# Grouped attention: which engine copies the transposed probabilities out of PSUM for units with two key tiles

## The chip, the cores and the metric

The kernel runs as one program on one core of a Trainium2 chip. The metric is the device time of that core in microseconds (us), lower is better. The core has five engines that matter here, each with its own in-order instruction queue: TensorE (PE, with its weight loads shown apart as PEld), VectorE (DVE), ScalarE (ACT), GpSimd (POOL) and SyncE (SP, which only issues transfers). They hand work to one another through semaphores: an instruction waits until a counter has reached a value, and adds to another counter when it is done.

## The reference, cut to what matters

The reference chains two small transformers of two layers each over 256 tokens of width 1024. The second one begins with a grouped-query attention layer (`gqa_axial_mixer`): 16 query heads share 4 key and value heads of width 64. The 256 tokens attend to 512 keys (256 of a context and their own 256); the 256 context tokens attend to the 256 context keys alone.

```
s = jnp.einsum('bqkgd,bskd->bkgqs', qi, k_all).astype(jnp.float32) * ATTN_SCALE
p = jax.nn.softmax(s, axis=-1).astype(v_all.dtype)
return jnp.einsum('bkgqs,bskd->bqkgd', p, v_all)
...
sc = jnp.einsum('bqkgd,bskd->bkgqs', qc, kc).astype(jnp.float32) * ATTN_SCALE
pc = jax.nn.softmax(sc, axis=-1).astype(vc.dtype)
oc = jnp.einsum('bkgqs,bskd->bqkgd', pc, vc).reshape(b, lc, A_WIDTH)
yc = (oc * jax.nn.silu(zc)) @ w_out
```

## The kernel before, in words

The whole kernel is one list of instructions for each engine, written out in order by hand; the layers follow each other, and nothing is scheduled at run time but by the semaphores. Four attention layers run through the same functions, named `attention` once in each engine's list, with a stage name: "l0", "l1", "a" (the grouped one, the only one that the change touches) and "b".

`attn_units(s)` cuts a stage into units. In stage "a" a unit is one pair of heads (t, from 0 to 7), one block of 128 queries (qt, 0 or 1) and one region: region 0 is the tokens, with 512 keys, four key tiles of 128; region 1 is the context, with 256 keys, two key tiles. The order is: for each t, for each qt, region 0 and then region 1. So there are 32 units; the even ones have four key tiles and the odd ones two. A job is the two units (qt 0 and 1) of one t and one region: units 12 and 14 are one job, units 13 and 15 the next. `AU0` and `AJ0` are the numbers of a stage's first unit and job among all stages.

A unit passes through these steps, each one or more rounds n after the other:

- PE, round n: two score products of unit n into PSUM tile A (`scores_a`, line 984).
- DVE, round n: the negated row maximum of unit n (line 1197), counted by `at_mx`.
- ACT, round n: two exponentials of unit n from PSUM into one of three SBUF buffers (tiles ATP, RSQ and HSQ, by unit modulo 3; line 1874), with row sums, counted by `at_ex`.
- DVE, round n + 1: `scaled`: a reciprocal of the sums (line 1172) and two multiplications of the probabilities (line 1182), counted by `at_p`.
- PE, round n + 2: `turn`: the transposes of the probabilities, 128 by 128 each, four or eight in all, into the PSUM tensor `RO` (tile R; line 636), counted by `at_t`. Before it PE waits that the unit's `at_p` is there and that the unit before has been copied out of `RO` (`at_tc`), for there is one `RO` for all units.
- ACT, round n + 2, ahead of the exponentials of unit n + 2: the copy of `RO` to SBUF (line 1863), to tile ATT for region 0 and to a part of tile B for region 1, counted by `at_tc`.
- PE, round n + 3, for the second unit of a job: the products with the values into PSUM tile G (`value_a`, line 993); in stage "a" they stand after that round's `turn`.
- DVE, round n + 4, for the second unit of a job: `out_a`, the product with the gate (line 1721); POOL then splits it into two parts for the next product.

Within a round PE's order is scores, `turn`, values; DVE's is maximum, `scaled`, `out_a`; ACT's is copy, exponentials.

Of the kernel before, what the change touches and what calls it, by code (L numbers as in the profile page):

```python
# [19 lines left out]
ACT = mybir.ActivationFunctionType  # L20
# [3 lines left out]
P = 128  # L24
# [87 lines left out]
AU0, AJ0 = {}, {}  # L112
# [7 lines left out]
def attn_units(s):  # L120

    out = []
    if s in ("l0", "l1"):
        for p in range(8):
            for qt in range(2):
                out.append((p, qt, qt + 1, p, qt == 1))
    else:
        regions = 2 if s == "a" else 1
        for t in range(8):
            for qt in range(2):  # L130
                for r in range(regions):
                    out.append((t, 2 * r + qt, 4 if r == 0 else 2, t * regions + r, qt == 1))
    return out


def program(nc, x_tok, wst, wmod, vec, cst, x_t, ctx_t, p_t, pos, pos4, tab, rpb, lam4, grow, y_t):
    with ExitStack() as ctx:
# [3 lines left out]
        def sem(name):  # L141
            return ctx.enter_context(nc.semaphore(name))
# [106 lines left out]
        def att(s, j):  # L249

            if s == "l0":
                return ATT[:, j % 2, 0:2, :].unsqueeze(1)
            if s == "l1":
                return ATT[:, j % 2, :, :].rearrange("p (l k) q -> p l k q", l=2)
            if j % 2 == 0:
                return ATT[:, :, :, :]
            spare = B[:, 4096:6144] if s == "a" else mv[:, 12288:14336]
            return spare.rearrange("p (l k q) -> p l k q", l=2, k=4)

        def lanes(a, nk):  # L260

            return AA[:, 1024 * (a % 2):1024 * (a % 2) + 1024].rearrange("p (l k) -> p l k", l=2)[:, :, 0:nk * P]
# [8 lines left out]
        def small(at, a, n):  # L271

            return SM[:, at + 2 * (a % 3):at + 2 * (a % 3) + n]
# [13 lines left out]
        def bc(ap, n):  # L287
# [4 lines left out]
        RO = ctx.enter_context(nc.psum_tensor("R", [P, 1024], F32))  # L292
# [21 lines left out]
        at_s, at_b, at_mx, at_ex, at_rc, at_lm, at_pa, at_p, at_t, at_tc, at_pv, at_g, at_oh, at_o = (  # L314
            sem("at_s"), sem("at_b"), sem("at_mx"), sem("at_ex"), sem("at_rc"), sem("at_lm"), sem("at_pa"), sem("at_p"),
            sem("at_t"), sem("at_tc"), sem("at_pv"), sem("at_g"), sem("at_oh"), sem("at_o"))
# [26 lines left out]
        n = 0  # L343
# [6 lines left out]
        n = 0  # L350
# [17 lines left out]
        def evacuated(eng, u):  # L368

            eng.wait_ge(bank_free[u % 2], u // 2 + 1)  # L370
# [732 lines left out]
        def _(dv):  # L1103
            v = nc.vector
# [60 lines left out]
            def scaled(s, n):  # L1165

                units = attn_units(s)
                nk = units[n - 1][2]
                a = AU0[s] + n - 1
                sm, rc = small(92, a, 2), small(98, a, 2)  # L1170
                dv.wait_ge(at_ex, 2 * (a + 1))
                v.reciprocal(rc, sm).then_inc(at_rc, 1)
                dv.wait_ge(at_rc, a + 1)
                if s == "l0":
                    p0, p1 = PRB[a % 3][:, 0, 0:nk * P], PRB[a % 3][:, 1, 0:nk * P]
                    v.tensor_scalar(p1, p1, rc[:, 1:2], LAM, ALU.mult, ALU.mult).then_inc(at_lm, 1)
                    dv.wait_ge(at_lm, a + 1)
                    v.scalar_tensor_tensor(p0, p0, rc[:, 0:1], p1, ALU.mult, ALU.add).then_inc(at_p, 1)
                else:
                    for c in range(2):  # L1180
                        pr = PRB[a % 3][:, c, 0:nk * P]
                        i = v.tensor_scalar(pr, pr, rc[:, c:c + 1], None, ALU.mult)
                        i.then_inc(at_p if c else at_pa, 1)

            def attention(s, bias, take_out=None, first=0, last=None, done=0):
                units = attn_units(s)
                for n in range(first, len(units) + 4 if last is None else last):
                    if n < len(units):
                        a = AU0[s] + n
                        sc = lanes(a, units[n][2])  # L1190
                        dv.wait_ge(at_s, a + 1)
                        b = bias(sc, units[n])
                        if b is not None:
                            biased[0] += 1
                            b.then_inc(at_b, 1)
                            dv.wait_ge(at_b, biased[0])
                        v.tensor_reduce(small(80, a, 2), sc, AX, ALU.max, negate=True).then_inc(at_mx, 1)  # L1197
                    if max(1, done + 1) <= n <= len(units):
                        scaled(s, n)
                    if take_out is not None and n >= 4 and units[n - 4][4]:  # L1200
                        un = units[n - 4]
                        j = AJ0[s] + un[3]
                        dv.wait_ge(at_pv, j + 1)
                        take_out(un, G[j % 2], j)
# [158 lines left out]
            def heads_rest(g):  # L1363

                for tt in range(2):
# [5 lines left out]
                                           ALU.subtract).then_inc(x_lo, 2)  # L1371

            attention("l0", bias_l0, None, 0, 16)
            heads_summed(0)
            attention("l0", bias_l0, None, 16)
            heads_applied(0)
            heads_summed(1)
# [203 lines left out]
            for u, (name, g, kt, panels) in enumerate(TOKEN):  # L1581
# [11 lines left out]
                if u == len(TOKEN) - 1:  # L1593
                    attention("l1", no_bias, None, 0, 2)
                    scaled("l1", 2)
# [71 lines left out]
            for u, (name, g, end) in enumerate(WIDE):  # L1667
# [3 lines left out]
                heads, width = (4, 256) if name == "kv" else (8, 512)  # L1671
# [144 lines left out]
        def _(ac):  # L1816
            act = nc.scalar.activation
# [28 lines left out]
            def load_table(function):  # L1846

                act(SM[:, warmed[0]:warmed[0] + 1], EPSC, function)
                warmed[0] += 1

            def attention(s, out=None, first=0, last=None):
                units = attn_units(s)
                width = 1 if s == "l0" else 2
                for n in range(first, len(units) + 4 if last is None else last):
                    if 2 <= n <= len(units) + 1:
                        p, qt, nk, job, last = units[n - 2]
                        a = AU0[s] + n - 2
                        j = AJ0[s] + job
                        ac.wait_ge(at_t, a + 1)
                        if j >= 2:  # L1860
                            ac.wait_ge(at_pv, j - 1)
                        q = qt % 2
                        act(att(s, j)[:, 0:width, 0:nk, q * P:(q + 1) * P],  # L1863
                            RO[:, :].rearrange("p (l k q) -> p l k q", l=2, k=4)[:, 0:width, 0:nk, :],
                            ACT.Copy).then_inc(at_tc, 1)
                    if n < len(units):
                        nk = units[n][2]
                        a = AU0[s] + n
                        sc = lanes(a, nk)
                        ac.wait_ge(at_mx, a + 1)  # L1870
                        if a >= 3:
                            ac.wait_ge(at_t, a - 2)
                        for c in range(2):
                            act(PRB[a % 3][:, c, 0:nk * P], sc[:, c, :], ACT.Exp, bias=small(80 + c, a, 1),
                                accum_out=small(92 + c, a, 1)).then_inc(at_ex, 1)
                    if n == len(units) and s == "a":
                        evacuated(ac, U0["a_z"] + 7)
                        act(Z2[:, 7, :], Z2[:, 7, :], ACT.Silu).then_inc(z_ok, 1)
                    if n == len(units) + (2 if s == "a" else 0):
                        load_table(ACT.Sqrt)  # L1880
                    if out is not None and n >= 4 and units[n - 4][4]:
                        j = AJ0[s] + units[n - 4][3]
                        ac.wait_ge(at_pv, j + 1)
                        out(units[n - 4], G[j % 2])
# [100 lines left out]
            def heads_out(g):  # L1985

                for tt in range(2):
                    ac.wait_ge(hn_tr, 2 * g + tt + 1)
                    act(XH[:, 8 + 4 * g:12 + 4 * g, tt * P:(tt + 1) * P], A[2 * g + tt].rearrange("p (k t) -> p k t", k=4),
                        ACT.Copy, scale=SUBG).then_inc(x_hi, 2)  # L1990

            attention("l0", out_l0, 0, 18)
            heads_root(0)
            attention("l0", out_l0, 18)
            heads_out(0)
            heads_root(1)
# [178 lines left out]
            for u, (name, g, kt, panels) in enumerate(TOKEN):  # L2175
# [9 lines left out]
                if u == len(TOKEN) - 1:  # L2185
                    attention("l1", None, 0, 2)
# [62 lines left out]
            for u, (name, g, end) in enumerate(WIDE):  # L2249
# [4 lines left out]
                heads, width = (4, 256) if name == "kv" else (8, 512)  # L2254
# [456 lines left out]
```

## Time and profile before

| what | value |
|---|---|
| time, median of 3 runs | 1334.96 us (1333.37 to 1335.37) |
| time of the profiled execution | 1335.48 us |
| its span in the trace | 1333.8 us |
| mean granted TensorE clock | 0.993 of full speed |
| PE, DVE, ACT, POOL busy, share of the span | 96%, 72%, 54%, 31% |
| stage "a", first scores to last transposes | about 963.7 to 1052.8 us of the span |

The span is what the trace covers; the time of the same execution is 1.68 us more. Engine busy times count instructions at work, not their waits. The rows that matter are shown in a section of their own below.

### The profile page before, as it was taken

The page shows a single profiled execution, that of the slowest core. Times are in us where ns is not written, and L with a number is a line of the kernel's source. Part 1 is how long each engine was busy: PE and PEld are TensorE (multiplying, and loading weights), DVE is VectorE, ACT ScalarE, POOL GpSimd, SP SyncE. Part 2 cuts the span into 40 slices and gives each one's busy share as a digit, 9 for nine tenths or more (in the row PEclk, how much of TensorE's full clock was granted, in tenths as well). Part 3 has the DMA queues.
Part 4 walks back from the last instruction along what each step waited for, and adds up shares of the span by engine and source line. Part 5 has one row for each costly group of instructions (what it writes and reads, how often), then busy time and mean ns, then how long its engine had stood idle before and what let it go on. Part 6 is the DMA issues. An engine that isn't in the chain of part 4 may idle for free.

```text
span 1333.8 us, 24373 instructions
## 1 busy us (share of the span) xinstructions
PE 1274.6 (96%) x8896; PEld 1104.8 (83%) x8896; DVE 954.7 (72%) x1426; ACT 720.5 (54%) x1249; POOL 411.8 (31%) x388
## 2 busy tenths in 40 slices
PE   6999999999999999999999999899989999999996
PEld 4887899999988877898999998788855599987656
DVE  6868688888878895558988887854277548453674
ACT  5555455555566777545565557444367515323562
POOL 4942234544433140143455443211012320000022
PEclk9999999999999999999999999899999999999999
DMA  8565246666744443155576664232200274522100
GB/s 308 188 215 179 80 155 224 216 226 209 232 143 143 159 141 95 61 191 174 193 236 212 228 207 146 95 108 85 90 17 1 49 179 137 174 96 79 48 1 32
DMA packets 52665, 191.72 MB, mean 144 GB/s; under 512 B 6048, under 2 KB 6304, under 8 KB 52320
## 3 DMA queue, kind: packets, MB, share of 16 engines
q1 hardware_dynamic: 43488, 158.59, 36.2%
q0 software_dynamic: 8368, 31.33, 7.5%
q8 instruction: 62, 1.02, 0.3%
q10 hardware_dynamic: 720, 0.57, 0.1%
q14 instruction: 27, 0.22, 0.1%
HBM read 189.41 MB, written 1.05 MB: 143 GB/s over the span
## 4 chain that ended last, share of the span: by engine, by line
PE 75%; DVE 11%; ACT 7%; issue 3%; POOL 2%; DMA 1%; SPq 0%; DVEq 0%; ACTq 0%; POOLq 0%
PE G L415 13%; PE G L417 13%; PE G L416 13%; PE A L415 5%; PE A L417 5%; PE A L416 5%; DVE WL L1116 4%; PE R L636 3%; ACT WH L1824 2%; PE R L563 2%; PE R L543 2%; PE R L415 1%; PE R L417 1%; PE R L416 1%; PE A L984 1%
## 5 line engine op out<-in xcount | busy, mean ns | idle before, releaser
L1116 DVE TENSOR_TENSOR WL<-RAW,WH 128x1024 fp32r<-128x1024 f32 x295 | 390.9, 1329 | 251.9 <-ACT WH L1824 251.5
L1824 ACT ACTIVATE WH<-RAW 128x1024 fp32r<-128x1024 f32 x295 | 310.7, 1057 | 394.9 <-PE G L417 282.8
L415 PE MATMUL G<-XH,WH 128*128 128x256 f32 (+1 forms) x1336 | 398.8, 298 | 6.4 <-DVE WL L1116 3.1
L416 PE MATMUL G<-XL,WH 128*128 128x256 f32 (+1 forms) x1336 | 395.5, 296 | 0.0
L417 PE MATMUL G<-XH,WL 128*128 128x256 f32 (+1 forms) x1336 | 395.5, 296 | 0.0
L415 PEld LDWEIGHTS G<-XH,WH 128*128 128x128 f32 x1336 | 256.0, 192 | 19.5 <-issue 8.4
L416 PEld LDWEIGHTS G<-XL,WH 128*128 128x128 f32 x1336 | 256.1, 192 | 7.4
L417 PEld LDWEIGHTS G<-XH,WL 128*128 128x128 f32 x1336 | 256.1, 192 | 6.3
L415 PE MATMUL A<-HH,WH 128*128 128x256 f32 x352 | 99.9, 284 | 1.3 <-POOL HL L2440 1.3
L416 PE MATMUL A<-HL,WH 128*128 128x256 f32 x352 | 99.6, 283 | 0.0
L417 PE MATMUL A<-HH,WL 128*128 128x256 f32 x352 | 99.5, 283 | 0.0
L2416 POOL CAST XH<-HRS 128x256 fp32r<-128x256 f32 x24 | 11.4, 475 | 267.3 <-DVE HRS L1721 267.3
L1197 DVE TENSOR_REDUCE SM<-A 128x2 f32<-128x1024 f32 (+1 forms) x80 | 67.7, 848 | 17.9 <-PE A L984 12.8
L415 PEld LDWEIGHTS A<-HH,WH 128*128 128x128 f32 x352 | 67.5, 192 | 2.9 <-ACT WH L1824 1.9
L415 PE MATMUL G<-WH,XH 128*128 128x512 f32 (+1 forms) x136 | 55.2, 406 | 13.9 <-DVE XL L1142 10.9
L1863 ACT ACTIVATE ATT<-R 128x1024 f32<-128x1024 f32 (+3 forms) x56 | 37.8, 674 | 56.7 <-PE R L636 56.7
L416 PEld LDWEIGHTS A<-HL,WH 128*128 128x128 f32 x352 | 67.5, 192 | 0.1
L417 PEld LDWEIGHTS A<-HH,WL 128*128 128x128 f32 x352 | 67.5, 192 | 0.0
L2436 POOL TENSOR_TENSOR HRS<-ATT,HRS 128x256 f32<-128x256 f32 x22 | 32.0, 1452 | 110.0 <-ACT HRS L2034 104.5
L415 PE MATMUL A<-WH,XH 128*128 128x512 f32 x144 | 58.4, 405 | 3.7 <-DVE XL L1454 1.9
L2436 POOL TENSOR_TENSOR HRS<-HSQ,HRS 128x256 f32<-128x256 f32 x22 | 32.0, 1453 | 94.3 <-ACT HRS L2034 94.3
L417 PE MATMUL A<-WH,XL 128*128 128x512 f32 x144 | 57.0, 396 | 0.0
(356 smaller groups left out, 2556.2 us busy)
## 6 DMA issues: line engine op xcount, KB each, us to landing
RAW<-in_wst SPq DMA_DIRECT2D x295, 512.0 KB, 4.0
M<-in_wmod POOLq DMA_DIRECT2D x48, 512.0 KB, 4.3
B<-in_rpb POOLq DMA_DIRECT2D x4, 1024.0 KB, 12.0
H<-in_x_t SPq DMA_DIRECT2D x2, 512.0 KB, 8.1
M<-in_x_tok SPq DMA_DIRECT2D x1, 1024.0 KB, 13.0
M<-in_ctx_t POOLq DMA_DIRECT2D x1, 1024.0 KB, 5.2
out_y<-M SPq DMA_DIRECT2D x2, 384.0 KB, 2.7
C<-in_cst SPq DMA_DIRECT2D x1, 737.0 KB, 15.1
```

The costliest lines, as they stand in the source:

```text
L415: mm(out, lh, rh, start=start, stop=False, skip_group_check=True)
L416: mm(out, lh, rl, start=False, stop=False, skip_group_check=True)
L417: return mm(out, ll, rh, start=False, stop=stop, skip_group_check=True)
L543: m = mm(out[32 * g:32 * g + 32, q * P:(q + 1) * P], SC[:, k, :], RM[:, i % RMS, k * P:(k + 1) * P], start=(k == 0), stop=(k == KD - 1), s ...
L563: m = mm(O[0:32, :], SCR[:, 2 * s + c, :], w[:, 512 * c:512 * c + 512], start=(s == 0 and c == 0 and w is RH), stop=(s == 3 and c == 1 and ...
L636: m = nc.tensor.transpose(ST[c][:, k * P:(k + 1) * P], PRB[a % 3][:, c, k * P:(k + 1) * P], IDT)
L984: m = mm(out[c][:, 0:nk * P], Q2[64 * c:64 * c + 64, t, qt * P:(qt + 1) * P], K2[64 * c:64 * c + 64, t // 4, k0:512], start=True, stop=Tru ...
L1116: v.tensor_tensor(WL[:, slot, :], RAW[:, raw, :], WH[:, slot, :].bitcast(F32), ALU.subtract).then_inc(w_lo, 1)
L1197: v.tensor_reduce(small(80, a, 2), sc, AX, ALU.max, negate=True).then_inc(at_mx, 1)
L1824: act(WH[:, slot, :], RAW[:, raw, :], ACT.Copy).then_inc(w_hi, 1)
L1863: act(att(s, j)[:, 0:width, 0:nk, q * P:(q + 1) * P], RO[:, :].rearrange("p (l k q) -> p l k q", l=2, k=4)[:, 0:width, 0:nk, :], ACT.Copy) ...
L2436: g.tensor_tensor(HID[b], CB[b][:, 0, :], SG[b], ALU.mult).then_inc(f_hid, 1)
```

## The change

For stage "a" alone, the copy of `RO` to SBUF of the odd units (two key tiles, 128 x 512 elements) is taken out of ACT's list and put into DVE's, as a `tensor_copy`. In DVE's round n it stands behind the maximum of unit n and `scaled` of unit n - 1, and ahead of `out_a` of unit n - 4; it copies unit n - 2. It waits for the same two counters as before (`at_t`, that the transposes are there, and `at_pv`, that the buffer written to has been read by the values of the job before last) and adds to the same `at_tc`. The even units (four key tiles, 128 x 1024) are copied by ACT as before, in the same place.

```
--- before.py
+++ after.py
@@ -1197,6 +1197,14 @@
                         v.tensor_reduce(small(80, a, 2), sc, AX, ALU.max, negate=True).then_inc(at_mx, 1)
                     if max(1, done + 1) <= n <= len(units):
                         scaled(s, n)
+                    if s == "a" and 2 <= n <= len(units) + 1 and units[n - 2][2] == 2:
+                        p, qt, nk, job, last = units[n - 2]
+                        a = AU0[s] + n - 2
+                        j = AJ0[s] + job
+                        dv.wait_ge(at_t, a + 1)
+                        dv.wait_ge(at_pv, j - 1)
+                        v.tensor_copy(att(s, j)[:, 0:2, 0:nk, (qt % 2) * P:(qt % 2 + 1) * P],
+                                      RO[:, :].rearrange("p (l k q) -> p l k q", l=2, k=4)[:, 0:2, 0:nk, :]).then_inc(at_tc, 1)
                     if take_out is not None and n >= 4 and units[n - 4][4]:
                         un = units[n - 4]
                         j = AJ0[s] + un[3]
@@ -1856,13 +1864,14 @@
                         p, qt, nk, job, last = units[n - 2]
                         a = AU0[s] + n - 2
                         j = AJ0[s] + job
-                        ac.wait_ge(at_t, a + 1)
-                        if j >= 2:
-                            ac.wait_ge(at_pv, j - 1)
                         q = qt % 2
-                        act(att(s, j)[:, 0:width, 0:nk, q * P:(q + 1) * P],
-                            RO[:, :].rearrange("p (l k q) -> p l k q", l=2, k=4)[:, 0:width, 0:nk, :],
-                            ACT.Copy).then_inc(at_tc, 1)
+                        if s != "a" or nk == 4:
+                            ac.wait_ge(at_t, a + 1)
+                            if j >= 2:
+                                ac.wait_ge(at_pv, j - 1)
+                            act(att(s, j)[:, 0:width, 0:nk, q * P:(q + 1) * P],
+                                RO[:, :].rearrange("p (l k q) -> p l k q", l=2, k=4)[:, 0:width, 0:nk, :],
+                                ACT.Copy).then_inc(at_tc, 1)
                     if n < len(units):
                         nk = units[n][2]
                         a = AU0[s] + n
```

## Rows read from the trace of the kernel before

**Rows 1.** The page, engines: busy us, share of the span, instructions.
```profile
PE 1274.6 (96%) x8896; PEld 1104.8 (83%) x8896; DVE 954.7 (72%) x1426; ACT 720.5 (54%) x1249; POOL 411.8 (31%) x388
```

**Rows 2.** Windows of stage "a", one per four units: first and last of five.
```profile
core 0: us, PE busy (x) PEld busy (x) DVE busy (x) ACT busy (x) POOL busy (x), PEclk, DMA share, GB/s
...
985.97:996.43 10.46, 9.67 (x65) 5.31 (x65) 7.78 (x19) 7.53 (x21) 2.25 (x5) 1.00 0.00 0
...
1027.78:1038.24 10.46, 9.67 (x65) 5.31 (x65) 7.79 (x19) 7.53 (x21) 2.26 (x5) 1.00 0.00 0
```

**Rows 3.** The chain that ended last, one period: start us, us, what.
```profile
1002.34 1.06 PE A L984 x4
1003.40 1.04 PE R L636 x8
...
1005.95 0.88 ACT RSQ L1874 x3
1006.88 1.13 PE A L984 x4
1008.01 1.09 PE R L636 x8
1009.12 1.03 ACT ATT L1863
1010.29 0.63 PE R L636 x4
1010.92 1.88 PE G L993 x16
1012.80 1.06 PE A L984 x4
```

**Rows 4.** Waits, 985.97 to 1038.24: waiter, releaser: us in total, times, longest.
```profile
ACT ATT L1863 <- PE R L636: 14.6, 10, 2.0
...
PE R L636 <- ACT ATT L1863: 2.9, 5, 0.6
```

**Rows 5.** Timeline of the same period: start us, us, instructions [idle before, releaser].
```profile
1004.46 1.02 ACT L1863 ACTIVATE ATT<-R 128x1024 f32<-128x1024 f32 x1 [2.03 <-PE R L636]
...
1006.71 0.61 ACT L1863 ACTIVATE B<-R 128x512 f32<-128x512 f32 x1
1006.86 0.17 DVE L1172 RECIPROCAL SM<-SM 128x2 f32<-128x2 f32 x1
...
1007.06 0.88 DVE L1182 TENSOR_SCALAR RSQ<-RSQ,SM 128x512 f32<-128x512 f32 x2
...
1007.86 0.42 DVE L1721 TENSOR_TENSOR HRS<-G,B 128x256 f32<-128x256 f32 x1
1007.99 0.86 PEld L636 LDWEIGHTS R<-C,RSQ 128*128 128x128 f32 x8 [0.82 <-DVE RSQ L1182]
...
1009.12 1.02 ACT L1863 ACTIVATE ATT<-R 128x1024 f32<-128x1024 f32 x1 [0.90 <-PE R L636]
...
1009.51 0.61 DVE L1182 TENSOR_SCALAR HSQ<-HSQ,SM 128x256 f32<-128x256 f32 x2
...
1010.26 0.42 PEld L636 LDWEIGHTS R<-C,HSQ 128*128 128x128 f32 x4 [0.94 <-DVE HSQ L1182]
...
1011.72 0.88 DVE L1182 TENSOR_SCALAR ATP<-ATP,SM 128x512 f32<-128x512 f32 x2
```

**Rows 6.** Groups by line and form, DVE copies from PSUM to SBUF: busy us, mean ns.
```profile
L1155 DVE COPY M<-G 128x512 f32<-128x512 f32 x8 | 5.5, 682 | 0.0
...
L1155 DVE COPY B<-G 128x512 f32<-128x512 f32 x1 | 0.7, 691 | 0.3 <-PE G L417 0.3
```

**Rows 7.** Timeline at the end of stage "a", PE and ACT.
```profile
1049.81 1.09 PE L636 MATMUL R<-C,HSQ 128*128 128x128 f32 x8 [1.33 <-DVE HSQ L1182]
...
1050.94 1.03 ACT L1863 ACTIVATE ATT<-R 128x1024 f32<-128x1024 f32 x1 [0.90 <-PE R L636]
```

**Rows 8.** Window ahead of stage "a" where the granted clock was lowest nearby.
```profile
850.00:860.00 10.00, 5.81 (x18) 3.96 (x17) 8.11 (x13) 3.19 (x8) 2.36 (x2) 0.71 0.16 49
```

## The prediction

> **What bounds the kernel now.** The engines' row of the page comes first: TensorE is busy 96% of the span, so over the whole kernel little but TensorE's own work sets the time [rows 1]. The change touches only the grouped stage, so the next view is the windows of that stage. It repeats every 10.46 us, one period for four units, and in each PE is busy 9.67 us, DVE 7.78 and ACT 7.53 [rows 2]. No engine is full there; what sets the 10.46 us is a loop of steps that wait for each other.
>
> The chain of waits shows the loop; I follow one period with its unit numbers [rows 3]. The scores of unit 14 (1002.34), the transposes of unit 12 (1003.40), then a stretch that the chain puts under "issue" and that is really ACT's copy of unit 12 (1004.46 to 1005.48) and the exponentials of unit 14, ending at 1006.83 [rows 3, 5]. They free the PSUM half that the scores of unit 16 write (1006.88). Then the transposes of unit 14 (1008.01), ACT's copy of unit 14 (1009.12), the transposes of unit 15 (1010.29), the values of the job of units 12 and 14 (1010.92), and at 1012.80 the scores of unit 18: 10.46 us on. Both ACT copies on this loop are those of even units, with four key tiles. The copies of odd units, which the change moves, are not on it.
>
> The waits say the same from ACT's side: before its ten even copies of five periods it sat idle 14.6 us for PE's transposes, up to 2.0 us at once; PE waited for a copy only five times, 2.9 us in all, each time an even one [rows 4]. ACT is not late.
>
> The timeline shows what DVE does meanwhile [rows 5]. The exponentials of unit 14 end at 1006.83; DVE takes the reciprocal at 1006.86 and the two multiplications from 1007.06 to 1007.94; the first weight load of unit 14's transposes starts at 1007.99, released by them. PE's scores of unit 16 run from 1006.88 to 1008.01. So unit 14's transposes have two conditions that come true within 0.05 us of each other: PE's own scores are done, and DVE's multiplications are done. DVE has no slack there.
>
> **The change part by part.**
>
> Removed from ACT: the copy of each odd unit, 0.61 us recorded (unit 13 at 1006.71), 16 in all [rows 5]. Worth nothing. Behind it on ACT stand the exponentials of unit 15, which then start when their maximum is there; but unit 15's next condition is at 1010.26, and ACT's next loop step, the copy of unit 14 at 1009.12, comes after 0.90 us of idling for PE. That idle time grows, no more. The other odd copy (unit 15) is followed by 2.03 us of the same idling, as the copy of unit 12 shows [rows 5].
>
> Added to DVE: the same copy, 128 x 512 fp32 from PSUM to SBUF. DVE's own copies of this form take 0.68 to 0.69 us [rows 6]; I take 0.69. In DVE's list the copy of unit 13 stands in round 15, behind the multiplications of unit 14 and ahead of the gate product of line 1721. Its two waits have long come true (ACT could start this copy at 1006.71), so it goes where the gate product now starts, at 1007.86, 0.08 before the recorded end of the multiplications, and ends at 1008.55.
>
> What waits for it: the transposes of unit 14, for they overwrite `RO`. Before, ACT had copied unit 13 by 1007.32, well ahead of 1007.99 [rows 5]. Now `RO` is free at 1008.55; with the 0.05 us that lie between a DVE end and the weight load (1007.94 to 1007.99) the transposes start at 1008.60 instead of 1007.99: **0.61 us late**. Queued behind them on PE are the scores of unit 17, the transposes of unit 15, the values and the scores of unit 18, all steps of the loop or fed by it; the copy of unit 14 on ACT and all that follows moves by the same 0.61. Nothing in the loop has room for it: the 0.58 us that PE idles ahead of unit 15's transposes (2.9 over five times, [rows 4]) ends with ACT's copy of unit 14, which is itself late.
>
> Queued behind it on DVE: the gate product, the maximum of unit 16 and the scaling of unit 15, all 0.61 later without a gap. The last is needed by unit 15's transposes: the multiplications ended at 1009.51 + 0.61 = 1010.12 and the weight load came at 1010.26 [rows 5]. Both move by 0.61, so the 0.14 us between them stays, 0.09 above the 0.05 of the handover. The gate product feeds POOL, busy 2.26 us of a period [rows 2]: free of charge.
>
> The second copy of the period, unit 15, stands behind the multiplications of unit 16 (1011.72 to 1012.60, [rows 5]). With the shift it ends at 1012.60 + 0.61 - 0.08 + 0.69 = 1013.82; with 0.05 for the handover, 1013.87. The transposes of unit 16 stood at 1012.80 + 1.06 = 1013.86 [rows 3] and now stand at 1014.47. So this one is hidden with 0.60 to spare: PE's values, 1.88 us, cover it. Without that cover it would cost another 0.69 a period.
>
> The two ends: the last odd units (29 and 31) behave alike. Unit 30's transposes at 1049.81 were released by DVE's multiplications [rows 7], with no scores beside them, and the copy of unit 29 now comes between: 0.61 again. The copy of unit 31 has the values of the job before and the first products of the next layer in front of its reader. After the stage PE goes back to matmuls that fill it (96% over the span, [rows 1]), so nothing later takes the delay back.
>
> **The sum**: eight head pairs, one late handover each, 8 x 0.61 = 4.9 us; I take 4.8, since at the first pair DVE starts from another state and may lose a little less. The profiled execution would go from 1335.48 to 1340.3 us. That execution lies 0.52 above the median of the runs, 1334.96, so the median forecast is **1339.8 us**.
>
> **Bounds of the added copy.** Below: nothing else is as cheap as ACT's own 0.61 for this shape [rows 5], which would make the shift 0.53, in all 4.2. Above: no overlap of 0.08 with the multiplications, and 0.1 more because unit 15's transposes have only 0.09 in hand: 0.79 a period, 6.3 in all. The value taken is that of the DVE rows of the same form.
>
> On the overlap the Trainium skill differs ("VectorE: DVE Perf Modes", "The DRAIN you can't avoid"): it has the next instruction of VectorE wait until the pipeline of the one before is empty. By that rule the shift would be 0.69 and the sum 5.5 us. The row shows the gate product starting 0.08 us ahead of the recorded end of the multiplications [rows 5], so I keep 0.61.
>
> **The rivals.**
>
> *No change to be measured.* The loads add up to less than a period: DVE's 7.78 plus two copies of 0.69 are 9.16 us of 10.46 [rows 2, 6], so if the two conditions of unit 14's transposes were looser than the rows say, for instance if the recorded end of the scores hid a backlog on PE, the copy would be hidden: 0 to 2.4 us (half the sum), 1335.0 to 1337.4. For it: matmul ends are modelled. Against: ACT's copy starts 1.11 us after the transposes in the chain (1008.01 to 1009.12), and 1.13 us after them at the end of the stage (1049.81 to 1050.94), where PE had idled 1.33 us before [rows 3, 7]; a backlog would make the first longer. This is also what the rule of occupancy in the Trainium skill would give ("Perfetto Trace Analysis", "Identifying the Most-Contended Engine"): none of the two engines becomes full. The rows speak against reading it so, for here the order in a queue decides. Chance 9%.
>
> *Faster.* ACT's queue is the limit, and 16 copies of 0.61 leave it: at most 9.8 us, 1325.2. It decides if ACT is late when the transposes of an even unit end. Against it stand 14.6 us of ACT idling in five periods [rows 4], so what could be gained is small. The Trainium skill's advice to share the evacuation of PSUM between both engines ("TensorEngine Tiling (Array Packing)", "PSUM Bottleneck") leads here. Chance 4%.
>
> *Slower than forecast.* A second wait joins: unit 15's scaling passes its 0.09 us, or the copy in this four-dimensional form is slower on DVE; 0.2 to 0.5 more per period gives 6.5 to 9 us, 1341.5 to 1344. Or the granted clock falls: PE's busy share in the stage goes from 9.67 / 10.46 = 0.92 to 9.67 / 11.07 = 0.87. Ahead of the stage a window with PE busy 5.81 of 10 us had a mean granted clock of 0.71, between the levels of 2.4 and 1.2 GHz [rows 8]; such a fall would cost up to 2.9 us, 1342.7. Against: 0.87 is far from 0.58. Chance 6%.
>
> **How the numbers follow.** The forecast has 81%, the others 9, 4 and 6. The forecast's own bounds are 1334.96 + 4.2 and + 6.3, that is 1339.2 to 1341.3; runs of one kernel lie up to 1.6 us from their median, which makes 1337.6 to 1342.9. That holds the forecast, the lower part of the slower case and the upper edge of the hidden one; I put the range at 1337.4 to 1342.6. What a measurement of this kernel can tell from no change is 0.2%, 2.7 us: slower begins at 1337.6. Slower: 81 + 6, with nothing of the hidden case: 0.87. Same: 0.09. Faster: 0.04.
>
> **What would show it.** In the profile after, the period of the grouped stage should be 11.07 us; the weight load of each unit 4t + 2's transposes should be released by DVE's copy, about 0.05 us after its end and some 0.6 after the end of the scores; the copy should be a 0.69 us DVE row; ACT should idle more ahead of its even copies, and PE should not wait for the copies of units 4t + 3. The prediction is wrong if the period stays at 10.46 (then the handover had slack), if DVE's copy is recorded well off 0.69, or if PE also waits for the scaling of unit 15 or the second copy.

## The result, and the profile of the changed kernel

The changed kernel takes 1341.08 us (median of six runs, 1340.58 to 1341.93) against 1334.85 for the kernel before in the same six rounds. The ratio is 1.0049, with a 95% interval of 1.0038 to 1.0059: slower by 5.1 to 7.9 us. Forecast were 1339.8 us within 1337.4 to 1342.6; the 4.8 us that were added for it lie just below the measured 5.1 to 7.9. The profiled execution took 1340.59 us, its span is 1338.9: 5.1 us above that of before.

The windows of the grouped stage, one per four units as in [rows 2], first and last of five:

```profile
core 0: us, PE busy (x) PEld busy (x) DVE busy (x) ACT busy (x) POOL busy (x), PEclk, DMA share, GB/s
985.00:996.12 11.12, 9.65 (x66) 5.31 (x66) 8.98 (x21) 6.67 (x20) 2.25 (x4) 1.00 0.00 0
...
1029.48:1040.60 11.12, 9.65 (x66) 5.31 (x66) 8.98 (x21) 6.67 (x20) 2.26 (x4) 1.00 0.00 0
```

The same work takes 11.12 us in place of 10.46. PE's work is what it was; DVE has 1.20 us more, ACT 0.86 less, and neither is full. The chain that ended last, over the same units as [rows 3], shows the step that came in (start us, us, what):

```profile
1004.12 1.06 PE A L984 x4
1005.18 1.04 PE R L636 x8
...
1007.16 1.45 ACT RSQ L1883 x4
1008.97 0.26 issue
1009.24 0.48 DVE RSQ L1182
1009.72 0.61 DVE B L1206
1010.46 1.08 PE R L636 x8
1011.56 1.03 ACT ATT L1872
1012.73 0.63 PE R L636 x4
1013.36 1.88 PE G L993 x16
1015.24 1.06 PE A L984 x4
```

Where the scores of unit 16 stood between the exponentials of unit 14 and the transposes of unit 14, there are now DVE's multiplications of unit 14 and its copy of unit 13 (line 1206). The rest of the loop is as before. The waits of five periods:

```profile
ACT ATT L1872 <- PE R L636: 22.2, 10, 2.5
...
PE R L636 <- DVE B L1206: 3.4, 5, 0.7
...
PE R L636 <- ACT ATT L1872: 2.9, 5, 0.6
```

ACT's idling ahead of its even copies grew from 14.6 to 22.2 us [rows 4]: of the 7.6 us, 4.3 are work that ACT no longer does (5 x 0.86), and 3.3 the longer periods (5 x 0.66). PE's wait for DVE's copy is new, once a period; its wait for ACT's copy of unit 14 is unchanged. The timeline of that period gives the handover:

```profile
1008.65 1.13 PE L984 MATMUL A<-M 64*128 64x512 f32 x4 [0.22 <-ACT RSQ L1883]
1008.83 0.88 DVE L1182 TENSOR_SCALAR RSQ<-RSQ,SM 128x512 f32<-128x512 f32 x2
...
1009.63 0.68 DVE L1206 COPY B<-R 128x512 f32<-128x512 f32 x1
...
1010.43 0.86 PEld L636 LDWEIGHTS R<-C,RSQ 128*128 128x128 f32 x8 [1.48 <-DVE RSQ L1182]
1010.46 1.06 PE L636 MATMUL R<-C,RSQ 128*128 128x128 f32 x8 [0.68 <-DVE B L1206]
...
1011.88 0.62 DVE L1182 TENSOR_SCALAR HSQ<-HSQ,SM 128x256 f32<-128x256 f32 x2
```

The copy starts 0.08 us before the recorded end of the multiplications (1009.71), as forecast, and takes 0.68 (mean 0.685 over the 16, the line below, from the groups by form). The copy ends at 1010.31; the first weight load of the transposes starts 0.12 us later, where 0.05 was forecast, and the first transpose 0.15 later.

```profile
L1206 DVE COPY B<-R 128x512 f32<-128x512 f32 x16 | 11.0, 685 | 1.3 <-PE R L636 1.3
```

### The profile page after: what moved, and what is told of

It reads as the page before. It is cut to its first block, busy times and chain, and to the rows that moved or that the text cites. A ratio compares the mean times of both kernels' runs of the same rounds, so it can differ in the third digit from the quotient of the medians.

```text
span 1338.9 us, 24373 instructions
## 1 busy us (share of the span) xinstructions
PE 1275.7 (95%) x8896; PEld 1104.4 (82%) x8896; DVE 965.9 (72%) x1442; ACT 713.9 (53%) x1233; POOL 412.9 (31%) x388
## 4 chain that ended last, share of the span: by engine, by line
PE 76%; DVE 11%; ACT 7%; issue 3%; POOL 1%; DMA 1%; DVEq 0%; SPq 0%; ACTq 0%; POOLq 0%
PE G L415 13%; PE G L417 13%; PE G L416 13%; PE A L415 6%; PE A L416 6%; PE A L417 6%; DVE WL L1116 4%; PE R L636 3%; ACT WH L1832 2%; PE R L563 2%; PE R L543 2%; DVE XL L1142 1%; PE R L415 1%; PE R L417 1%; PE R L416 1%
## 5 line engine op out<-in xcount | busy, mean ns | idle before, releaser
L416 PE MATMUL A<-WL,XH 128*128 128x512 f32 x144 | 58.5, 406 | 0.0
```

What stands on the lines that cost most here:

```text
L416: mm(out, lh, rl, start=False, stop=False, skip_group_check=True)
```

## The experiments

Each ratio is against runs of the kernel before on the same chip in the same rounds. "Period" is the time from the scores of unit 4t + 2 to those of unit 4t + 6, as in [rows 3].

**Which of the two copies costs.** In the first kernel DVE takes only the copies of units 4t + 1, in the second only those of units 4t + 3:

```
-  if s == "a" and 2 <= n <= len(units) + 1 and units[n - 2][2] == 2:
+  if s == "a" and 2 <= n <= len(units) + 1 and (n - 2) % 4 == 1:      # second kernel: == 3
...
-  if s != "a" or nk == 4:
+  if s != "a" or (n - 2) % 4 != 1:                                     # second kernel: != 3
```

> Only the copies of units 4t+1 go to VectorE; those of units 4t+3 stay on ScalarE. Theory of the handover (the one late step is the transposes of unit 4t+2, which wait for the copy of unit 4t+1 behind VectorE's multiplications): the period of the grouped stage is that of the changed kernel, 11.12 us against 10.46 before, and the time is 5 us above before. Rival, load (each copy that VectorE takes over costs alike): half of it, a period of 10.79 and 2.6 us.

Measured: 1341.86 us against 1333.80, ratio 1.0055 (1.0041 to 1.0068). The chain has the scores of units 14 and 18 at

```profile
1003.86 1.06 PE A L984 x4
1014.98 1.06 PE A L984 x4
```

a period of 11.12: the whole loss.

> Only the copies of units 4t+3 go to VectorE. Theory of the handover: hidden behind the products with the values, period 10.46, no change from before. Rival, load: a period of 10.79 and 2.6 us more.

Measured: 1334.60 against 1333.80, ratio 1.0003 (0.9994 to 1.0012), period 10.45:

```profile
1003.22 1.06 PE A L984 x4
...
1013.67 1.06 PE A L984 x4
```

In its timeline the copy of unit 15 and the transposes that need it:

```profile
1013.39 0.68 DVE L1206 COPY B<-R 128x512 f32<-128x512 f32 x1
...
1014.66 1.09 PE L636 MATMUL R<-C,ATP 128*128 128x128 f32 x8
```

The copy ends at 1014.07, 0.59 us before these transposes start. The forecast of 0.60 had 0.05 for the handover taken off, so it stands for 0.65 counted this way. The second copy is hidden, the first costs everything, and "each copy costs alike" is out.

**DVE busy, nobody waiting.** ACT copies everything, as before; DVE does an extra product of constants in the place of the copy. This adds work that the reference doesn't ask for and leaves nothing out.

```
 scaled(s, n)
+if s == "a" and n % 4 == 3:
+    v.tensor_tensor(HRS[:, :, T:2 * T], COS_SIN, COS_SIN, ALU.mult)   # COS_SIN: 128 x 512 constants, C[:, CC["cos2"]:...]
```

> ScalarE copies all units as before; VectorE does a product of 128 x 512 fp32 of constants, about 0.69 us, which nobody reads and nobody waits for, in the place of the copy of unit 4t+1. Theory of the handover taken alone (only PE's wait for the copy costs): no change, period 10.46. Rival, queue (what stands behind the copy in VectorE's list is late as well): the scaling of unit 4t+3 is 0.61 us late and passes the 0.09 us that its transposes have in hand, so these start 0.52 us later, period 10.98, 4.2 us above before.

Measured: 1337.76 against 1333.80, ratio 1.0031 (1.0019 to 1.0043), and the period is 10.98, as the rival on the queue had it:

```profile
1002.45 1.06 PE A L984 x4
...
1013.43 1.06 PE A L984 x4
```

Its timeline:

```profile
1007.96 0.69 DVE L1201 TENSOR_TENSOR HRS<-C 128x512 f32<-128x512 f32 x1
...
1008.10 1.09 PE L636 MATMUL R<-C,RSQ 128*128 128x128 f32 x8
...
1010.22 0.62 DVE L1182 TENSOR_SCALAR HSQ<-HSQ,SM 128x256 f32<-128x256 f32 x2
...
1010.89 0.66 PE L636 MATMUL R<-C,HSQ 128*128 128x128 f32 x4 [1.06 <-DVE HSQ L1182]
```

The transposes of unit 14 (1008.10) are not late, for nobody needs the product. The multiplications of unit 15 are, and its transposes idle 1.06 us for them, where they idled 0.57 for ACT's copy. So 0.52 of the 0.66 us a period is lost by DVE's occupation alone: by this, a second `RO` buffer, which would take away PE's wait alone, would save 0.14 us a period; that is an estimate, and it wasn't tried. In the changed kernel the two losses don't add up, because the late transposes of unit 14 move the next condition along with them.

**The handover.** PE's two waits ahead of a unit's transposes, in the other order, in the changed kernel:

```
-pe.wait_ge(at_p, a + 1)
 if a >= 1:
     pe.wait_ge(at_tc, a)
+pe.wait_ge(at_p, a + 1)
```

> The changed kernel, with TensorE's two waits ahead of a unit's transposes in the other order: first that RO is free, then that the probabilities are there. In the trace after, the transposes of unit 4t+2 start 0.15 us after VectorE's copy ends, where 0.05 was forecast. Theory that the place of the wait sets this (the one that stands last is answered sooner): the handovers of unit 4t+2 and of unit 4t+3 each become about 0.08 us shorter, period 10.95, about 1.3 us below the changed kernel. Rival, the delay lies with the copy itself: period 11.12 as in the changed kernel.

Measured: 1339.44 against 1333.80, ratio 1.0038 (1.0025 to 1.0052), period 1014.80 - 1003.77 = 11.03. Between the two expectations:

```profile
1009.28 0.69 DVE L1206 COPY B<-R 128x512 f32<-128x512 f32 x1
...
1010.02 0.86 PEld L636 LDWEIGHTS R<-C,RSQ 128*128 128x128 f32 x8 [1.42 <-DVE B L1206]
```

The copy ends at 1009.97 and the first weight load follows in 0.05 us, where the changed kernel needed 0.12: for DVE's copy the order of the waits is worth 0.07. Ahead of unit 15's transposes it is worth 0.02, and the two make the 0.09 that the period lost:

```profile
1011.15 1.02 ACT L1872 ACTIVATE ATT<-R 128x1024 f32<-128x1024 f32 x1 [1.86 <-PE R L636]
...
1011.54 0.61 DVE L1182 TENSOR_SCALAR HSQ<-HSQ,SM 128x256 f32<-128x256 f32 x2
...
1012.27 0.42 PEld L636 LDWEIGHTS R<-C,HSQ 128*128 128x128 f32 x4 [0.92 <-ACT ATT L1872]
```

ACT's copy ends last, at 1012.17, and the profile names it. But the wait for unit 15's multiplications is now the second; they end at 1012.15, and the weight load follows 0.12 later, the answer of a second wait. At unit 3 of the stage, where the multiplications end 0.35 us ahead of ACT's copy, the weight load follows the copy in 0.05 (979.12 to 979.17). So both handovers follow the order of the waits. The view of line 633, which holds the second wait in both kernels, shows over the stage (960 to 1060) that it is an instruction of its own on PE's queue, once for each of the 32 units and 51 ns long; the line of the first wait has none. In the changed kernel:

```profile
L633 PEldq EVENT_SEMAPHORE  x32: 51/51/51, 968.7 to 1057.1; - x32
```

In time the gain can't be told from the changed kernel.

**What holds unit 15's transposes.** The prediction saw two conditions 0.09 us apart there. Three kernels built on the one before take them away. The swap on DVE:

```
+early = s == "a" and n % 4 == 0 and done + 1 <= n < len(units)
+if early:
+    scaled(s, n)                    # unit n - 1, ahead of the maximum of unit n
...
-if max(1, done + 1) <= n <= len(units):
+if max(1, done + 1) <= n <= len(units) and not early:
     scaled(s, n)
```

> The kernel before, with one swap in VectorE's list: in round 4t+4 the scaling of unit 4t+3 stands ahead of the maximum of unit 4t+4. Theory of two conditions (the transposes of unit 4t+3 wait for ScalarE's copy of unit 4t+2 and, 0.09 us less late, for this scaling): the copy still decides, period 10.46, no change. Rival, VectorE alone holds these transposes: they start up to 0.57 us sooner, period 9.89, 4.6 us below before.

Measured: 1334.05 against 1334.86, ratio 0.9998 (0.9989 to 1.0007), period 1011.62 - 1001.16 = 10.46, as the theory of two conditions had it.

The cut of ACT's copy of units 4t + 2, shortened here, without PE's part, which waits for each half of `RO` by itself:

```
 if halves(s, n - 2):
+    ac.wait_ge(at_th, half_no(n - 2))          # first head's four transposes done
...
+    act(first half of RO -> att).then_inc(at_tf, 1)
+    ac.wait_ge(at_t, a + 1)
+    act(second half of RO -> att).then_inc(at_tc, 1)
```

> The kernel before, with ScalarE's copy of unit 4t+2 cut in two, one for each head of the pair, each starting when its half of the transposes is done, and the next transposes waiting half by half. Theory of two conditions: the copy no longer decides, the scaling on VectorE does, and only 0.09 us a period is won: period 10.37, 0.7 us below before, hardly to be told from none. Rival, the copy alone holds them: period 9.89, 4.6 us below before.

Measured: 1334.05 against 1334.86, ratio 0.9993 (0.9984 to 1.0002). The releaser of unit 15's transposes changed from ACT's copy to DVE, and the period became 10.38 (1009.59 - 999.21 between these transposes):

```profile
1009.59 0.66 PE L650 MATMUL R<-C,HSQ 128*128 128x128 f32 x4 [0.46 <-DVE HSQ L1198]
```

> Both at once, on the kernel before. Theory of two conditions: the transposes of unit 4t+3 follow the scores of unit 4t+5 without a gap, 0.57 us a period is won, period 9.89, 4.6 us below before (0.9966). Rival, some third step fills the gap: period 10.3 or more.

Measured: 1331.86 against 1334.86, ratio 0.9976 (0.9966 to 0.9986): two edits that alone can't be told from no change gain 0.24% together. The period is 1008.75 - 998.60 = 10.15, less gain than expected. Its timeline shows what took the rest:

```profile
1004.73 0.40 POOL L2444 CAST XH<-HRS 128x256 fp32r<-128x256 f32 x1 [1.39 <-DVE HRS L1740]
1004.85 1.24 DVE L1198 TENSOR_SCALAR HSQ<-HSQ,SM 128x256 f32<-128x256 f32 x2
...
1005.20 0.73 POOL L2446 TENSOR_TENSOR XL<-HRS,XH 128x256 fp32r<-128x256 f32 x1
...
1007.25 0.69 ACT L1902 ACTIVATE ATP<-A,SM 128x512 f32<-128x512 f32 x1 [1.09 <-DVE SM L1216]
```

The multiplications of unit 15 take 1.24 us, where [rows 5] has 0.61 for the same two. GpSimd splits a gate product beside them, in a conversion and a subtraction, and they end 0.16 us after the subtraction's recorded end at 1005.93. The kernel with the swap alone has the same 1.24 (1007.27 to 1008.51); there unit 15's transposes, which wait for ACT's copy until 1009.08, hide it. The maximum of unit 16 behind them is late, its exponentials and with them the scores of unit 18.

> As split and swap together, with the copies of units 4t cut in two as well. Theory: the exponentials of unit 4t+2 start about 0.3 us sooner, the 0.21 us that TensorE idles ahead of the scores of unit 4t+4 goes as well, period 9.68, TensorE full, 6.2 us below before (0.9954). Rival, the second half copy delays ScalarE as much as the earlier start gains: period 9.89 as with the other two alone.

Measured: 1331.02 against 1334.86, ratio 0.9969 (0.9957 to 0.9981), period 1007.94 - 997.92 = 10.02, for the same reason: the multiplications take 1.12.

**The slow multiplications.** The gate product of the second job (line 1721 of before) goes behind the maximum in round 4t + 4, one round later, but for the last pair:

```
+behind = 1 if s == "a" and n >= 5 and units[n - 5][1] == 3 and n - 5 < len(units) - 1 else 0   # [1] == 3: unit 4t + 3
+here = n - 4 - behind
+if s == "a" and not behind and n >= 4 and n - 4 < len(units) - 1 and units[n - 4][1] == 3:
+    here = -1
-if take_out is not None and n >= 4 and units[n - 4][4]:
-    un = units[n - 4]
+if take_out is not None and here >= 0 and units[here][4]:
+    un = units[here]
```

> As the kernel with both even copies cut and the swap (period 10.02), with VectorE's gate product of the second job of a pair moved behind the maximum of unit 4t+4, so that GpSimd's split of it no longer runs beside the scaling of unit 4t+3. In the kernel without the move this scaling's two multiplications took 1.12 us, where 0.62 was the rule, while GpSimd was at work. Theory (GpSimd's work beside them slows them, and this made the maximum of unit 4t+4, its exponentials and so the scores of unit 4t+6 late): they take 0.62 again, the scores of unit 4t+6 come when TensorE is free, about 0.1 us sooner, period 9.9, 1 us below the kernel without the move and 4.5 below before. Rival, the multiplications are slow for another reason: they stay at 1.1, period 10.02.

Measured: 1329.25 against 1334.38, ratio 0.9955 (0.9941 to 0.9969), period 9.70, more than expected:

```profile
999.75 1.06 PE A L1000 x4
...
1009.45 1.06 PE A L1000 x4
```

and in its timeline

```profile
1005.84 0.62 DVE L1198 TENSOR_SCALAR HSQ<-HSQ,SM 128x256 f32<-128x256 f32 x2
...
1006.92 0.65 PE L650 MATMUL R<-C,HSQ 128*128 128x128 f32 x4
```

The multiplications take 0.62 again and unit 15's transposes follow PE's scores without idling. That the gate product is gone from ahead of them gives them no earlier start: in both kernels unit 15's reciprocal starts 0.44 us after unit 14's multiplications end (1003.51 to 1003.95 without the move, 1005.20 to 1005.64 with it). This version beats both kernels; PE is busy 9.86 of 10 us in the stage.

**The part that the first trace doesn't explain.** The trace has 5.1 us, the medians differ by 6.2. The two profiled executions alone account for that: the one of before lay 0.63 us above the median of its runs, the one of the changed kernel 0.49 below. What is open is whether this is mere scatter. In the trace of the kernel with units 4t + 1 alone the granted clock fell near the end of the stage. So the changed kernel was run once more, and once with the copy of unit 29 given back to ACT:

```
-... and units[n - 2][2] == 2:
+... and units[n - 2][2] == 2 and n - 2 != 29:
```

> The changed kernel once more, for its times and a second trace. The first trace explains 5.1 us, the medians differ by 6.2. In the traces of two relatives of it (odd copies of units 4t+1 on VectorE) TensorE idled 2.0 us ahead of the last pair's transposes of unit 30, and then the granted clock fell for 3.4 us, which cost 1.6 us; in the first trace of the changed kernel it did not fall there. Theory (the clock falls there in some executions): times in the range 1340.5 to 1342, that is 5.1 us above before without and 6.7 with the fall. Rival (only scatter): 5.1 us above, whatever the clock does there.

Measured: 1340.82 against 1334.02, ratio 1.0051 (1.0038 to 1.0065), 5.1 to 8.7 us, which holds both expectations. The windows from 1055 to 1060 us, of the first trace of the changed kernel, of the second trace, and of the kernel with units 4t + 1 alone (the column before the last two is the mean granted clock):

```profile
1055.00:1060.00 5.00, 5.00 (x36) 3.58 (x37) 2.45 (x6) 3.92 (x4) 1.14 (x2) 1.00 0.01 2
```

```profile
1055.00:1060.00 5.00, 5.00 (x29) 3.61 (x27) 1.30 (x2) 4.47 (x6) 0.46 (x1) 0.71 0.01 2
```

```profile
1055.00:1060.00 5.00, 5.00 (x26) 3.86 (x26) 1.27 (x2) 3.73 (x5) 1.04 (x2) 0.66 0.00 0
```

A mean of 0.71 is part of the window at 1.2 GHz and the rest at 2.4. Two microseconds of the second trace lie almost wholly at the lower level:

```profile
1056.00:1058.00 2.00, 2.00 (x7) 1.42 (x6) 0.00 (x0) 1.97 (x3) 0.00 (x0) 0.51 0.00 0
```

From the stage's first scores to its last gate product the first trace needs 1062.36 - 963.55 = 98.81 us, the second 1063.00 - 962.61 = 100.39 and the kernel with units 4t + 1 also 1063.68 - 963.29 = 100.39: the fall costs 1.58 us. In all of them PE had idled 2.0 us ahead of unit 30's transposes, in the kernel before 1.33 [rows 7], and there the clock stayed, as in the eight other traces, with 1.34 us or less.

> The changed kernel with one copy, that of unit 29, given back to ScalarE. By the handover alone the last pair's 0.66 us come back. Theory (the clock falls in some executions after TensorE's long wait ahead of unit 30's transposes): that wait is 1.3 us as before, the clock stays, and 0.7 to 2.3 us come back, on the whole some 1.7 below the changed kernel. Rival (only scatter): 0.7 below.

Measured: 1339.69 against 1334.02, ratio 1.0040 (1.0027 to 1.0054). Its stage takes 1061.88 - 963.72 = 98.16 us, 0.65 less than the first trace, and its clock stayed at 1.00 there. The time lies 1.1 us below the changed kernel, between 0.7 and 1.7, and the intervals overlap: it doesn't decide how often the clock falls.

## Why the prediction was right, point by point

**The removed copies were worth nothing**: shown for those of units 4t + 3, without which ACT's queue gives the same period (10.45 against 10.46); for those of units 4t + 1 it is read off ACT's idling, 7.6 us more in five periods, and no run takes them away alone.

**The first copy is the late step**: shown by the kernels with one copy each, a period of 11.12 against 10.45. The 0.05 us that the prediction sees between the two conditions of unit 14's transposes are only the handover behind DVE; DVE released them already [rows 5], so its condition was the later one and had nothing in hand. **The second is hidden with 0.60 to spare**: shown; 0.59 counted to the start of the transposes, where the forecast comes to 0.65, with one copy and in the changed kernel alike.

**What lies behind it on DVE moves along, and unit 15's scaling stays just in time**: shown. In the changed kernel it ends at 1012.50, 0.23 before its transposes, which wait for ACT's copy as before. The filler kernel shows that this condition is real: without the late transposes of unit 14 it decides by itself.

**The size** was off by one term, the handover. 0.61 a pair was 0.69 - 0.08 for the copy, with the 0.05 us to the weight load that PE had needed after DVE's multiplications. The copy ends 0.60 after the multiplications, and the weight load comes 0.12 after it, 0.07 more than forecast; from there to ACT's copy of unit 14 1.13 us pass, as before (1007.99 to 1009.12 [rows 5], 1010.43 to 1011.56). That makes 0.67, and the period grew by 0.66. The rows of before had the right figure: the wait for `RO` is the second one, and ahead of unit 15's transposes, where it decided, ACT's copy ends at 1010.14 and the weight load starts at 1010.26 [rows 5]. The prediction took the 0.05 of the first wait. The reserve for the first pair was wrong: its transposes of unit 2 came 12.91 us after the first scores before and 13.56 after, 0.65 late like the others. Eight pairs give 5.3 us; the stage grew from 1057.27 - 963.72 = 93.55 to 98.81, by 5.26, in place of 4.8. The median of 1341.08 lies inside the forecast's own bounds as well, 1339.2 to 1341.3, but near the upper one, and that is in part luck: what the upper bound was made of, no overlap with the multiplications and a late scaling of unit 15, did not happen; the handover, and then scatter or the clock, brought it there.

**The clock**: the prediction gave a fall a small chance, since PE's share over the whole stage stays at 0.87. Around the last pair PE is busy 2.97 of 5 us (1050 to 1055 of the first trace), with 2.0 of idling in one piece, and of two traces of the changed kernel one has the fall, at 1.58 us where up to 2.9 was the bound. With it the 5.3 us of the stage become 6.8, and the measured 5.1 to 7.9 lie around the two. That a mixture of both makes the median is argued, not shown: scatter would do it as well, and the mean granted clock listed for each run, 0.993 or 0.994 in all six, is too coarse to tell (1.58 of 1339 us are some 0.001 of it).

**The rivals**: "no change" and "faster" are out by the ratio. The Trainium skill's occupancy rule ("Perfetto Trace Analysis", "Identifying the Most-Contended Engine") names neither DVE, busy 8.98 of 11.12 us, nor ACT as full; the trace shows that here the order within a queue sets the time. Its rule that the next VectorE instruction waits for an empty pipeline ("VectorE: DVE Perf Modes", "The DRAIN you can't avoid") gave 5.5 us, near the stage's 5.3, but the copy starts 0.08 us before the recorded end of the multiplications here too, and what is missing lies in the handover. The same section adds that a next instruction which is not held starts earlier, so the row doesn't contradict it.

## What to carry to other kernels

Work taken from an engine that idles ahead of its part of a loop gave nothing back here; first see which of its instructions stand on the chain. Before putting an instruction into another in-order queue, write down for each thing behind it, and for each one waiting on it, how much time it has in hand: here none for the transposes of unit 14, which DVE already released, and 0.09 us for the scaling of unit 15, and a 0.69 us copy passed both. Take the price of a handover from a row with the same wait in the same place. Where two conditions come true almost together, take both away in one edit; here one alone showed no change (ratios of 0.9998 and 0.9993).

## What the runs showed of the hardware that was not expected

DVE's fp32 multiplications from SBUF to SBUF (128 x 256, two of them) take 0.61 to 0.62 us alone and 1.12 to 1.24 while GpSimd splits 128 x 256 elements beside them. They end 0.15 to 0.16 us after the subtraction that is the second step of the split (swap alone: 1008.36 and 1008.51; both edits: 1005.93 and 1006.09; both copies cut: 1005.12 and 1005.27); moved apart they take 0.62 again. The subtraction takes 0.72 to 0.75 us either way. The kernel before has it too, at the last unit of the stage: the two multiplications take 1.24 us (1050.27 to 1051.51), and the subtraction ends at 1051.37. The Trainium skill says that VectorE, in a mode that uses both of its SBUF ports, and GpSimd exclude each other at a shared pair of ports ("SBUF — State Buffer", "Who interferes with whom"); the numbers agree, though no run here shows the mode, and the profile shows the blocking only as a longer instruction, with no wait.

PE's answer to a semaphore depends on which of two waits is written second: the weight load follows the release 0.12 us later if that wait is the second and 0.05 if it is the first, for copies by DVE and by ACT alike. The second wait is recorded as an instruction of its own, 51 ns long.

After 1.9 to 2.0 us of PE idling the granted clock fell to the 1.2 GHz level in three of four traces with that idling (the changed kernel once of twice, the kernel with units 4t + 1, the one with the waits exchanged), and 1.58 us were lost after the wait itself had been paid. In the nine traces with 1.34 us or less at that place it stayed at 1.00.
